# All branch gates through the front Strassen stage, both branch projections as a token-major Strassen stage

## The chip, the cores and the metric

One core of one Trainium2 chip. The metric is the device time of one execution of the whole program in microseconds (us). The kernel before takes 2709.2 us, the median of three runs (2709.17 to 2709.56).

## What is computed

One layer of a streaming encoder, 512 tokens wide (T), 2048 channels deep (D), all in float32:

```python
h = rmsnorm(x, norm_mix)
proj = h @ w_in
q_a, f_a, i_a, g_a, q_b, k_b, v_b, gate_a, gate_b = jnp.split(proj, IN_OFFSETS, axis=-1)
o_a = hgrn2_mixer(q_a, f_a, i_a, g_a, lb, hg_norm)      # 8 heads of 128: recurrence
o_b = swa_mixer(q_b, k_b, v_b, positions, sw_sinks)     # 16 query heads of 64, 4 key heads, window 128
merged = sigmoid(gate_a) * (o_a @ w_proj_a) + sigmoid(gate_b) * (o_b @ w_proj_b)
x = x + merged @ w_out
x = x + cross_attn(rmsnorm(x, norm_x), rmsnorm(mem, norm_mem))
x = x + (silu(hf @ w_gate) * (hf @ w_up)) @ w_down      # hf = rmsnorm(x, norm_ffn)
return rmsnorm(x, norm_final)
```

`w_proj_a` and `w_proj_b` are 1024x2048, `w_out` is 2048x2048, and each gate is 2048 channels wide.

## The kernel before

**Products.** A float32 product is made of three reduced products: each operand is split into a high part (a copy rounded to fp32r) and a low part (the rest), and `products` (L1024) issues low x high, high x low and high x high. ScalarE makes the high parts (`split_hi` L1733), GpSimd the low parts of the plainly computed weights (`split_lo` L917), VectorE those of the Strassen stages (`front_low`, `out_low_part`, `f_low`). Plain weights run through a ring of four slots (`w_raw`, `w_hi`, `w_lo`), one slot for a 128x1024 piece, a *chunk* of 24 matmuls with 512 columns (`chunk` L1034).

**Order.** Each engine has one instruction stream written out by hand; semaphores join them. SP issues the loads and GpSimd the accumulating loads, in the order in which each is written, so that a load stands behind every wait before it in its queue.

**Front stage** (`front_chunk` L1125, `front_high` L1803, `front_low` L2565, `front_combine` L2581). Part of `h @ w_in` is done as a Strassen product of 2x2 blocks: seven products in place of eight, each of 4 chunks of 12 matmuls, 28 chunks to a group of 1024 columns. There are NF = 4 groups: the first makes the values of branch A, groups 1 to 3 make 12 of the 16 column tiles of each gate. VectorE and ScalarE combine the blocks (`front_keep` L1840, `front_combine`), and SP stores them, not yet through the sigmoid, in DRAM (`front_store` L666).

**Heads.** The recurrence of the 8 heads follows (`head` L1188, L1920, L2622). In the last two head steps, which have no projections of their own, the four plain gate A tiles fill TensorE (`gate_ahead` L1184).

**Gate stage A** (`gate_stage` L1295, L1995; `gate_loads` L736; `gate_product` L2808). Sixteen times, one 128-column tile of `o_a @ w_proj_a` is computed with 24 matmuls, channels on partitions. For 12 of them the stored gate rows are loaded and turned by four transposes on TensorE, ScalarE takes the sigmoid, and VectorE writes gate times projection into `res`. Inside this stage, at tile 14, VectorE computes the angles of the rotary embedding (`rope_angles` L2792).

**Window attention** (L1380 to L1395; ScalarE from L2038; VectorE from L2855). 12 tiles of the projection: four of keys and values, each followed by its two tiles of queries, 48 matmuls each. Scores, softmax and values of a tile pair run in the middle of later chunks. At the end two plain gate B tiles stand.

**Gate stage B** is the same as A with `w_proj_b`; `merge` (L2892) adds to `res`. The other two plain gate B tiles stand in it.

**w_out** (`out_chunk` L1421, `out_high` L2068, `out_low_part` L2903, operands at L2086, L2918, L2936) is a Strassen stage of 56 chunks of 12 matmuls, with the channel-major `res` as its stationary side. Then come cross-attention, the feed-forward network and the last norm, which the change leaves alone but for semaphore names.

Of the kernel before, what the change touches and what calls it, by code (L numbers as in the profile page):

```python
# [24 lines left out]
P = 128  # L25
D = 2048
T = 512
# [27 lines left out]
C_K, C_V, C_H, C_GA, C_S, C_GB, C_XQ, C_XO, C_F = 0, 8, 16, 64, 88, 112, 136, 144, 152  # L55
# [3 lines left out]
NF = 4  # L59
FRONT = 28 * NF  # L60
FRONT_SETS = [(0, 2, 1), (1, 2, 0)] * (NF // 2)
PLAIN = 4
GATED = KT - PLAIN

# [14 lines left out]
def gate_chunk(m, stage):  # L79
    return (4, 7)[m] if m < 2 and stage else 8 + m  # L80
# [20 lines left out]
F0, TOTALS = FRONT, 4 * NF + OUT_SUMS  # L101
# [79 lines left out]
def build_trunk(nc, a, out):  # L181

    ctx = ExitStack()
    with ctx:
# [19 lines left out]
        res = at("res", 64 * KB, [P, KT, T], F32)  # L204
# [4 lines left out]
        o_lo = at("o_lo", 112 * KB, [P, HEADS, T], F32R)  # L209

# [47 lines left out]
        gate_t = at("gate_t", SCR + 25.5 * KB, [P, 2, T], F32)  # L258

        eps_col = stat[:, 31:32]  # L260
        gate_rows = at("gate_rows", SCR + 16 * KB, [P, 4, TT, P], F32)

# [37 lines left out]
        pos_i = at("pos_i", SCR + 12 * KB, [P, T], I32)  # L300
# [5 lines left out]
        out_last = [at(f"out_last{x}", (32 + 4 * x) * KB, [P, 2 * 512], F32) for x in range(4)]  # L306
        out_low = [at(f"out_low{x}", (48 + 4 * x) * KB, [P, 2 * 512], F32) for x in range(4)]
# [89 lines left out]
        gate_dram = nc.dram_tensor("gate_scratch", [2, TT, P, GATED * P], F32, kind="Internal").ap()  # L397
# [56 lines left out]
        def front_loaded(x, c, count):  # L454
            earlier = sum(1 for s in range(C_H + HC) if s % RING == c) if x == 0 else 0
            return 16 * (earlier + count)

# [71 lines left out]
        def front_block(n, p, c):  # L529

            left = BLOCK[p] in ("b11", "b21")
            c0 = I_A + (0 if left else 512) if n == 0 else (GATE_A if left else GATE_B) + 512 * n
            k0 = 2 * c + (0 if BLOCK[p] in ("b11", "b12") else CK)
            return w_rows[:, k0:k0 + 2, c0:c0 + 512]
# [15 lines left out]
        def front_freed(x):  # L550
            return max(i for i in range(FRONT) if front_slot(i) == x) + 1

# [20 lines left out]
        def w_slot_freed(eng, s):  # L573

            if C_XQ <= s < C_XQ + RING:
                last = max(k for k in range(NO) if k % RING == s % RING)
# [7 lines left out]
        def _(sp):  # L584
# [53 lines left out]
            for c in range(4):  # L638
                front_load(0, 5, c)
# [13 lines left out]
            for c in range(4):  # L653
                sp.wait_ge(w_lo_ready, max(s for s in range(C_H + HC) if s % RING == c) + 1)
                front_load(0, 0, c)
# [10 lines left out]
            def front_store(n, name):  # L666
# [5 lines left out]
                else:  # L672
                    sp.wait_ge(S("f_combined"), made(n, name))
# [62 lines left out]
            def gate_loads(gate0, w_proj, s0, stage):  # L736

                def project(m0, s, v=0, k=0):
                    unit(w_proj, m0, s, v, k, chunks=1)

                for m in range(2 if stage else PLAIN):
                    unit(w_in, gate0 + m * P, s0 + 2 * m)
                for m in range(2):
                    project(m * P, s0 + gate_chunk(m, stage))
                    if stage:
                        unit(w_in, gate0 + (2 + m) * P, s0 + gate_chunk(m, stage) + 1)
                if stage:
                    sp.wait_ge(S("sw_o_done"), HEADS)
                else:
                    sp.wait_ge(S("o_split"), HEADS)  # L750
                    for name in ("11", "12", "21", "22"):
                        sp.wait_ge(S(STORES[name]), front_stored(NF - 1))
                with sp.Fori(0, 3) as i:
                    for x in range(4):
                        project(i * (4 * P) + (2 + x) * P, s0 + gate_chunk(2 + x, stage), i, 4)
                        sp.wait_ge(S("turned"), i * 4 + (2 * KT + GATED * stage + x - 3))
                        sp.sem_inc(S("slot_free"), 1)
                        rows = gate_dram[stage][:, :, bass.ds(i * (4 * P) + x * P, P)].rearrange("t p d -> p t d")
                        sp.dma_start(gate_rows[:, x], rows).then_inc(S(f"x_in{x}"), 16)
                project(14 * P, s0 + gate_chunk(14, stage))  # L760
                project(15 * P, s0 + gate_chunk(15, stage))

            gate_loads(GATE_A, a["w_proj_a"].rearrange("l d n -> (l d) n"), C_GA, 0)
            for g in range(SWKV):
                s = C_S + 6 * g
# [7 lines left out]
                for x in range(2):  # L773
                    unit(w_in, Q_B + (2 * g + x) * P, s + 2 + 2 * x)
            gate_loads(GATE_B, a["w_proj_b"].rearrange("l d n -> (l d) n"), C_GB, 1)
# [5 lines left out]
            for j in range(4):  # L781
                sp.wait_ge(w_lo_ready, C_XQ - RING + j + 1)
                out_load(0, 0, j // 2, j % 2)
            sp.wait_ge(chunk_done, C_GB + 22)
# [23 lines left out]
            sp.wait_ge(S("x_o_done"), XH)  # L808
# [105 lines left out]
        def _(pool):  # L914
            pool.memset(ones[:, :], 1.0).then_inc(S("ones_set"), 1)
# [27 lines left out]
            for s in range(C_GA + LEAD, C_GA + RING):  # L943
                pool.wait_ge(w_lo_ready, s)
                split_lo(s)
            with pool.Fori(C_GA // RING + 1, C_XQ // RING) as i:
                for s in range(RING):
                    split_lo(s, i, RING)

# [73 lines left out]
        def _(pe):  # L1023
# [43 lines left out]
            for u in range(XH):  # L1067
# [5 lines left out]
                if u == 2:  # L1073

                    pe.wait_ge(S("ones_set"), 1)
# [49 lines left out]
            def front_chunk(i):  # L1125

                n, p, c = front_step(i)
                o = (pair[(0, 3)[n % 2]], pair[1], pair[(0, 3)[n % 2]], pair[1], pair[(0, 3)[n % 2]], pair[2], pair[(0, 3)[n % 2]])[p]
# [2282 lines left out]
```

## Time and profile before

| | |
|---|---|
| median of three runs | 2709.2 us |
| the profiled execution, span of its trace | 2707.3 us |
| TensorE busy | 2680.3 us (99%), 12902 matmuls |
| VectorE, ScalarE, GpSimd busy | 62%, 48%, 22% |
| DMA | 441.57 MB, 163 GB/s on average |

Busy time of an engine is the time in which an instruction of it runs; TensorE's matmuls are pipelined, so their own durations overlap, and the distance between two of them is read from a count in a stretch. Of each wait the profile names what ended it.

### The profile page before, as it was taken

What the parts mean: (1) busy time and instruction counts of PE and PEld (TensorE: products, weight loads), DVE (VectorE), ACT (ScalarE), POOL (GpSimd) and SP (SyncE); (2) the same over time, 40 slices, a digit from 0 to 9 for tenths busy, and PEclk for the clock granted to TensorE, in tenths of its full rate; (3) what the DMA queues carried; (4) which work ended last, traced back from release to release, by engine and by line L of the source; (5) the groups of instructions that cost most, each with busy time, mean ns of one, the idle gap of its engine ahead of it and who ended that gap; (6) DMA issues with size and microseconds to landing.
All of it is one profiled execution on the core that took longest, in us unless ns stands there. A gap on an engine that the chain in (4) does not pass through costs nothing.

```text
span 2707.3 us, 33905 instructions
## 1 busy us (share of the span) xinstructions
PE 2680.3 (99%) x12902; PEld 2225.3 (82%) x12902; DVE 1683.3 (62%) x2031; ACT 1306.9 (48%) x1634; POOL 601.6 (22%) x394
## 2 busy tenths in 40 slices
PE   8999999999999999999999999999999999999998
PEld 7878888888888888878887888888888888888887
DVE  5865557777413541488558556666555667778787
ACT  6544445545423552345455544444444445545446
POOL 7121110000233334311141221111122212121311
PEclk9999999999999999999999999999999999999999
DMA  8788884222153323586348787877778888898975
GB/s 279 207 197 199 191 186 114 86 83 83 55 160 93 79 79 111 158 214 147 110 148 216 169 176 166 192 179 171 178 166 177 170 217 193 198 209 236 188 213 134
DMA packets 356893, 441.57 MB, mean 163 GB/s; under 512 B 30265, under 2 KB 200593, under 8 KB 354193
## 3 DMA queue, kind: packets, MB, share of 16 engines
q1 hardware_dynamic: 277120, 286.23, 34.0%
q0 software_dynamic: 76704, 147.87, 31.9%
q10 hardware_dynamic: 2928, 5.56, 0.6%
q8 instruction: 93, 1.52, 0.2%
q14 instruction: 48, 0.39, 0.0%
HBM read 407.36 MB, written 32.24 MB: 162 GB/s over the span
## 4 chain that ended last, share of the span: by engine, by line
PE 88%; DMA 4%; issue 3%; DVE 3%; POOL 1%; ACT 1%; SPq 0%; DVEq 0%; POOLq 0%; ACTq 0%
PE psum L1027 17%; PE psum L1029 17%; PE psum L1028 17%; PE psum L1409 9%; PE psum L1410 9%; PE psum L1411 9%; PE psum L1160 2%; PE psum L1161 2%; PE psum L1162 2%; DMA f_raw<-in_w_down 1%; PE psum L1210 1%; PE psum L1649 1%; DMA f_raw<-in_w_out 1%; DMA fr_raw<-in_w_in 1%; DVE x_nat L2504 0%
## 5 line engine op out<-in xcount | busy, mean ns | idle before, releaser
L3132 DVE TENSOR_TENSOR f_lo<-f_raw,f_hi 128x1024 fp32r<-128x1024 f32 x458 | 559.4, 1225 | 398.2 <-ACT f_hi L2246 397.0
L2246 ACT ACTIVATE f_hi<-f_raw 128x1024 fp32r<-128x1024 f32 x460 | 486.8, 1061 | 620.6 <-PE psum L1411 311.6
L922 POOL TENSOR_TENSOR w_lo<-w_raw,w_hi 128x1024 fp32r<-128x1024 f32 x103 | 250.9, 2446 | 702.5 <-ACT w_hi L1739 700.4
L981 POOL DMA_DIRECT2D f_raw<-in_w_up x132 | 159.0, 1205 | 661.9 <-DVE f_lo L3132 656.2
L1027 PE MATMUL psum<-op_hi,w_lo 128*128 128x512 f32 x704 | 284.2, 404 | 0.0
L1029 PE MATMUL psum<-op_hi,w_hi 128*128 128x512 f32 x704 | 274.8, 390 | 0.0
L1028 PE MATMUL psum<-op_lo,w_hi 128*128 128x512 f32 x704 | 274.6, 390 | 0.0
L2568 DVE TENSOR_TENSOR fr_lo<-fr_raw,fr_hi 128x1024 fp32r<-128x1024 f32 x112 | 137.0, 1225 | 125.0 <-ACT fr_hi L1815 125.0
L1815 ACT ACTIVATE fr_hi<-fr_raw 128x1024 fp32r<-128x1024 f32 x112 | 118.5, 1061 | 167.4 <-PE psum L1162 82.4
L1739 ACT ACTIVATE w_hi<-w_raw 128x1024 fp32r<-128x1024 f32 x152 | 158.8, 1054 | 40.2 <-PE psum L1029 16.2
L1029 PEld LDWEIGHTS psum<-op_hi,w_hi 128*128 128x128 f32 x704 | 132.1, 188 | 28.5
L1027 PEld LDWEIGHTS psum<-op_hi,w_lo 128*128 128x128 f32 x704 | 132.5, 188 | 25.8 <-issue 0.9
L1028 PEld LDWEIGHTS psum<-op_lo,w_hi 128*128 128x128 f32 x704 | 132.6, 188 | 24.5 <-issue 0.2
L1000 POOL DMA_DIRECT2D f_raw<-in_w_down x70 | 86.0, 1444 | 285.6 <-DVE f_lo L3132 277.4
L1409 PE MATMUL psum<-f_hi,pa_lo 128*128 128x512 f32 x352 | 137.2, 390 | 0.6 <-DVE f_lo L3132 0.6
L1409 PE MATMUL psum<-f_hi,s_lo 128*128 128x512 f32 x352 | 137.0, 389 | 0.0
L1411 PE MATMUL psum<-f_hi,s_hi 128*128 128x512 f32 x352 | 137.0, 389 | 0.0
L1410 PE MATMUL psum<-f_lo,pa_hi 128*128 128x512 f32 x352 | 137.0, 389 | 0.0
L1410 PE MATMUL psum<-f_lo,s_hi 128*128 128x512 f32 x352 | 136.9, 389 | 0.0
L1411 PE MATMUL psum<-f_hi,pa_hi 128*128 128x512 f32 x352 | 136.9, 389 | 0.0
L1027 PE MATMUL psum<-f_hi,a_lo 128*128 128x512 f32 x344 | 134.8, 392 | 0.0
L1029 PE MATMUL psum<-f_hi,a_hi 128*128 128x512 f32 x344 | 134.0, 390 | 0.0
(438 smaller groups left out, 6282.8 us busy)
## 6 DMA issues: line engine op xcount, KB each, us to landing
f_raw<-in_w_up POOLq DMA_DIRECT2D x132, 512.0 KB, 6.5
f_raw<-in_w_gate SPq DMA_DIRECT2D x88, 512.0 KB, 4.2
w_raw<-in_w_in SPq DMA_DIRECT2D x80, 512.0 KB, 4.0
f_raw<-in_w_down POOLq DMA_DIRECT2D x70, 512.0 KB, 8.9
f_raw<-in_w_down SPq DMA_DIRECT2D x66, 512.0 KB, 5.6
fr_raw<-in_w_in SPq DMA_DIRECT2D x48, 512.0 KB, 4.6
fr_raw<-in_w_in POOLq DMA_DIRECT2D x48, 512.0 KB, 7.1
f_raw<-in_w_up SPq DMA_DIRECT2D x44, 512.0 KB, 4.6
```

The lines of the kernel that those rows point to most:

```text
L922: pool.tensor_tensor(w_lo[:, slot], w_raw[:, slot], w_hi[:, slot].bitcast(F32), ALU.subtract).then_inc(w_lo_ready, 1)
L981: pool.dma_start(raw_pieces(x, slot), up_block(n, p, c), accum_op=ALU.add).then_inc(raw_added[c], 16)
L1027: pe.matmul(b[:, 0:n], wl, xh, start=start, stop=False)
L1028: pe.matmul(b[:, 0:n], wh, xl, start=False, stop=False)
L1029: return pe.matmul(b[:, 0:n], wh, xh, start=False, stop=stop)
L1409: pe.matmul(b, lo[:, kt, f], w[0], start=False, stop=False, skip_group_check=True)
L1410: pe.matmul(b, hi[:, kt, f], w[1], start=False, stop=False, skip_group_check=True)
L1411: return pe.matmul(b, hi[:, kt, f], w[0], start=False, stop=stop, skip_group_check=True)
L1739: act.activation(w_hi[:, slot], w_raw[:, slot], ACT.Copy).then_inc(w_hi_ready, 1)
L2246: act.activation(f_split(i)[0][:, :], split_source(i)[:, :], ACT.Copy).then_inc(f_hi_ready, 1)
L2568: dve.tensor_tensor(fr_lo[front_slot(i)][:, :], front_source(i)[:, :], fr_hi[front_slot(i)][:, :].bitcast(F32), ALU.subtract).then_inc(f_l ...
L3132: dve.tensor_tensor(lo[:, :], split_source(i)[:, :], hi[:, :].bitcast(F32), ALU.subtract).then_inc(f_lo_ready, 1)
```

## The change

- **Gates.** NF = 5: all 16 tiles of each gate go through the front stage, 512 columns of gate A and 512 of gate B to a group. ScalarE takes the sigmoid there (`open_gate`), before the store. No plain gate tile is left, and the 24 x 4 transposes of gate rows go.
- **Keys ahead.** The four key/value tiles fill the last two head steps in place of the gate A tiles; ScalarE keeps them in `kv_raw`. The window attention that follows has the 8 query tiles alone. `rope_angles` stands on VectorE directly behind the last head.
- **Mixed stage.** Both projections become one Strassen stage with tokens on partitions: NG = 4 groups (side A and B, two column halves of 1024 each), each of 7 products x 2 chunks (YC = 14) of 12 matmuls. The stationary blocks and sums of `o_a`, `o_b` are made on VectorE (side A) and on GpSimd (most of side B). The sums of weight blocks are made in SBUF by GpSimd (`sum_blocks`, eight of 128x1024 a group). VectorE makes the low part of each chunk, the combinations, and gate times projection into `rows_m`. The rest of the window attention stands between the first five mixed chunks.
- **One turn.** The merged rows are turned once for `w_out`: 32 transposes between chunks of mixed group 3, 32 behind the first four chunks of `w_out` (`turn_merged`); ScalarE copies them into `res` (`merged_keep`).
- `w_out` uses its ring slots in another order (`out_slot`), and several semaphores are joined or renamed.

The diff, cut to its core:

```diff
-NF = 4
+NF = 5
...
+NG, YC = 4, 14
+MIXED = NG * YC
...
+def mixed_slot(i):
+    return (0, 2, 3)[i % FR]
+
+
+def out_slot(k):
+    return (3, 0, 2, 1)[k % RING]
...
+            def sum_blocks(o, other, waits):
+                for semaphore, count in waits:
+                    pool.wait_ge(semaphore, count)
+                pool.tensor_tensor(o[:, :], o[:, :], other[:, :], ALU.add).then_inc(S("m_summed"), 1)
...
+            for n in range(NG):
+                for c in range(2):
+                    sum_blocks(m_tot[n % 2][c], m_b12[c], ((f_lo_ready, mixed_at(n, 0) + c + 1), (S("m_b12_in"), 32 * (n + 1))))
+                for c in range(2):
+                    sum_blocks(m_tot[n % 2][c], m_b22[c], ((f_lo_ready, mixed_at(n, 1) + c + 1), (S("m_b22_in"), 32 * (n + 1))))
+                if n == 0:
...
+                    next_difference(ma_run, OA12, "m_raw")
+                if n == 1:
...
+                    difference(mb_run, OB21, OB22, "m_raw")
+                if n == 2:
+                    difference(mb_last, OB11, OB21, "m_last_raw")
+                for c in range(2):
+                    sum_blocks(m_b22[c], m_b12[c], ((f_lo_ready, mixed_at(n, 3) + c + 1),))
+                for c in range(2):
+                    sum_blocks(m_tot[n % 2][c], m_b21[c], ((f_lo_ready, mixed_at(n, 2) + c + 1), (S("m_b21_in"), 32 * (n + 1))))
...
+            def mixed_chunk(i):
+
+                n, p, c = mixed_step(i)
...
+                pe.wait_ge(f_lo_ready, FRONT + i + 1)
+                hi, lo = MIXED_STAT[n // 2][p]
+                for j in range(2):
+                    kt = 2 * c + j
...
+                    for t in range(2):
+                        xh, xl = [x[:, kt, t * P:(t + 1) * P] for x in (hi, lo)]
+                        if p in (0, 1, 5):
+                            last = products(o[:, t], 512, (xh, xl), (wh, wl), kt == 0, kt == 3)
...
+            def turn_merged(kt, b):
+                for t in range(TT):
+                    last = pe.transpose(bank[b][:, t * P:(t + 1) * P], rows_m[:, t, kt * P:(kt + 1) * P], ident[:, :])
+                last.then_inc(S("merged_turned"), 1)
...
+            mixed_chunk(0)
+            sw_turn(HEADS - 2)
+            sw_scores(HEADS - 1)
+            mixed_chunk(1)
+            sw_values(HEADS - 2)
+            mixed_chunk(2)
+            mixed_chunk(3)
+            sw_turn(HEADS - 1)
+            mixed_chunk(4)
+            sw_values(HEADS - 1)
...
             for k in range(NO):
                 out_chunk(k)
+                if k < 4:
...
+                    for y in range(2):
...
+                        turn_merged((12, 14, 8, 10)[k] + y, (2, 2, 0, 0)[k] + y)
...
+            def open_gate(n, name):
+
+                tile = FRONT_TILES[name]
+                act.wait_ge(S("f_combined"), made(n, name))
+                act.activation(tile[:, :, :], tile[:, :, :], ACT.Sigmoid).then_inc(S("gate_open"), 1)
...
-            gate_stage(C_GB, KT, 1)
             out_operand_high(0)
             out_high(0)
+            for x in (8, 9):
+                merged_keep(x)
             out_high(1)
+            for x in (10, 11):
+                merged_keep(x)
             out_operand_high(1)
...
             for k in range(2, NO):
                 out_high(k)
+                if k in (2, 3):
+                    for x in (8 + 2 * k, 9 + 2 * k):
+                        merged_keep(x)
...
+            dve.memset(kT_pad[:, 0:64], 0.0)
+            dve.memset(vT_pad[:, 0:64], 0.0)
+            rope_angles()
...
+            def gate_side(n, name, tile):
...
+                if n < 2:
+                    dve.wait_ge(S("gate_in"), 16 * 8)
+                    dve.tensor_tensor(o, o, tile, ALU.mult).then_inc(S("m_gated"), 1)
+                else:
...
+                    link(dve.tensor_tensor(g, g, tile, ALU.mult))
+                    dve.tensor_tensor(o, o, g, ALU.add).then_inc(S("m_gated"), 1)
...
+            for i in range(6, MIXED):
+                mixed_low(i)
+                mixed_outputs(i)
```

## Rows read from the trace of the kernel before

**Rows 1.** The page's first part: busy time, share of the span, instructions.

```profile
PE 2680.3 (99%) x12902; PEld 2225.3 (82%) x12902; DVE 1683.3 (62%) x2031; ACT 1306.9 (48%) x1634; POOL 601.6 (22%) x394
```

**Rows 2.** Waits of TensorE: us in total, times, longest.

```profile
PE psum L1409 <- DVE f_lo L2907: 1.3, 2, 1.0
```

**Rows 3.** Stretches: length, busy PE PEld DVE ACT POOL, clock, DMA share, GB/s.

```profile
0.00:10.00 10.00, 2.79 (x13) 2.68 (x14) 1.15 (x4) 3.18 (x7) 0.40 (x5) 1.00 0.77 245
200.00:360.00 160.00, 160.00 (x708) 132.47 (x707) 86.61 (x72) 70.28 (x68) 30.09 (x25) 1.00 0.85 198
741.00:1120.00 379.00, 379.00 (x2188) 311.32 (x2187) 118.35 (x221) 145.48 (x302) 146.20 (x62) 1.00 0.39 107
1137.00:1184.00 47.00, 45.14 (x196) 36.02 (x195) 36.83 (x33) 21.42 (x22) 14.47 (x12) 1.00 0.91 193
2700.00:2707.00 7.00, 0.00 (x0) 0.00 (x0) 1.94 (x7) 1.97 (x5) 0.00 (x0) 0.70 0.73 300
```

**Rows 4.** Chain that ended last: start, us, what.

```profile
741.41 0.86 PE psum L1261 x2
...
1500.02 0.87 PE psum L1649 x8
```

**Rows 5.** The page's part 5: costliest groups, VectorE and ScalarE.

```profile
L3132 DVE TENSOR_TENSOR f_lo<-f_raw,f_hi 128x1024 fp32r<-128x1024 f32 x458 | 559.4, 1225 | 398.2 <-ACT f_hi L2246 397.0
...
L1815 ACT ACTIVATE fr_hi<-fr_raw 128x1024 fp32r<-128x1024 f32 x112 | 118.5, 1061 | 167.4 <-PE psum L1162 82.4
```

**Rows 6.** Timelines of VectorE, ScalarE, GpSimd, 745 to 853 us: start, us, what.

```profile
745.95 0.69 DVE L2754 TENSOR_TENSOR o_lo<-o_t,o_hi 128x512 fp32r<-128x512 f32 x1 [0.78 <-ACT o_hi L1961]
...
772.69 2.39 POOL L922 TENSOR_TENSOR w_lo<-w_raw,w_hi 128x1024 fp32r<-128x1024 f32 x1 [3.54 <-ACT w_hi L1739]
...
835.85 0.11 DVE L2826 MEMSET kT_pad<- 128x64 f32 x1
...
846.12 0.43 DVE L2806 TENSOR_SCALAR turns<-q_rot 128x512 f32<-128x512 f32 x1
...
846.58 0.63 ACT L2024 ACTIVATE cos_t<-turns 128x512 f32<-128x512 f32 x1 [3.73 <-DVE turns L2806]
...
851.52 0.59 ACT L2059 ACTIVATE vT_pad<-psum 64x512 f32<-64x512 f32 x1 [2.41 <-PE psum L1029]
...
852.13 1.19 ACT L2063 ACTIVATE swapped_t<-psum 32x512 f32<-32x512 f32 x2
```

**Rows 7.** Timelines of TensorE, VectorE, ScalarE, 884 to 901 us: one tile pair's attention.

```profile
884.39 1.10 PE L1334 MATMUL psum<-kT_pad,q_rot 64*64 64x128 f32 x32
...
892.57 0.69 DVE L2852 TENSOR_TENSOR probs_t<-probs_t,sw_small 128x512 f32<-128x512 f32 x1
...
898.57 1.15 PE L1353 MATMUL psum<-probs_T,v_win 128*64 128x64 f32 x32
...
899.77 0.60 ACT L2051 ACTIVATE o_hi<-psum 128x512 fp32r<-128x512 f32 x1 [2.33 <-PE psum L1353]
```

**Rows 8.** Timelines of VectorE and GpSimd, 1387 to 1408 us.

```profile
1387.90 2.48 DVE L2968 TENSOR_TENSOR x_row<-x_row,psum 128x512 f32<-128x512 f32 x4 [2.96 <-PE psum L1029]
...
1389.10 2.41 POOL L922 TENSOR_TENSOR w_lo<-w_raw,w_hi 128x1024 fp32r<-128x1024 f32 x1 [3.03 <-ACT w_hi L1739]
...
1390.30 5.77 DVE L2995 TENSOR_TENSOR h_nat<-x_row,g_row 128x512 f32<-128x512 f32 x4
...
1393.11 2.41 POOL L972 TENSOR_TENSOR first_lo<-f_raw,first_hi 128x1024 fp32r<-128x1024 f32 x1 [1.60 <-ACT first_hi L2246]
...
1406.62 1.29 DVE L2995 TENSOR_TENSOR h_nat<-x_row,g_row 128x512 f32<-128x512 f32 x2
```

**Rows 9.** Timeline of TensorE, 3 to 24 us.

```profile
7.50 3.68 PE L1062 MATMUL psum<-ident,mem_nat 128*128 128x128 f32 x16 [4.29 <-DMA mem_nat<-in_mem]
...
16.13 0.41 PE L1027 MATMUL psum<-mem_hi,w_lo 128*128 128x256 f32 x1
...
17.00 0.28 PE L1027 MATMUL psum<-mem_hi,w_lo 128*128 128x256 f32 x1
```

More of the change, by code:

```diff
@@ L575, in w_slot_freed @@
             if C_XQ <= s < C_XQ + RING:
-                last = max(k for k in range(NO) if k % RING == s % RING)
+                last = max(k for k in range(NO) if out_slot(k) == s % RING)
                 eng.wait_ge(f_chunk_done, F0 + last + 1)
@@ L734, in _ @@
                     head_loads(i * 2 + (2 + x), C_H + 2 * HC + HC * x, x, i, 2 * HC)
[L736 to L763, printed above, removed]
             for g in range(SWKV):
-                s = C_S + 6 * g
+                s = C_KV + 2 * g
                 for j in range(2):
@@ new lines, in _, with pool_link, plain, difference @@
+            pool_links = [1]
+            def pool_link(ins):
+                ins.then_inc(S("pool_step"), 1)
+                pool_links[0] += 1
+                pool.wait_ge(S("pool_step"), pool_links[0])
+            def plain(block):
+                return [t.bitcast(F32) for t in block]
+            def difference(o, one, other, signal):
+                (hi1, lo1), (hi2, lo2) = plain(one), plain(other)
+                pool_link(pool.tensor_tensor(o[:, :, :], hi1, hi2, ALU.subtract))
+                pool_link(pool.tensor_tensor(o[:, :, :], o[:, :, :], lo1, ALU.add))
+                pool.tensor_tensor(o[:, :, :], o[:, :, :], lo2, ALU.subtract).then_inc(S(signal), 1)
@@ new lines, in swap_halves, with swap_keys @@
+            def swap_halves(src, m, rows):
+                before(act, S("q_roped"), m - (m + 2) // 3)
+                before(act, S("k_roped"), (m + 2) // 3)
+                for r in range(0, rows, 32):
+                    last = act.activation(swapped[r ^ 32:(r ^ 32) + 32, :], src[r:r + 32, :], ACT.Copy)
+                last.then_inc(S("halves_swapped"), 1)
+            def swap_keys(g):
+                before(act, S("windows_turned"), g)
+                act.wait_ge(S("lb_shifted"), 1 + 2)
+                act.activation(vT_pad[64:128, 64:64 + T], kv_raw[g][64:128, :], ACT.Copy).then_inc(S("vT_padded"), 1)
+                swap_halves(kv_raw[g], 3 * g, 64)
@@ new lines, in _ @@
+            for n in range(HEADS):
+                if n >= 2:
+                    turned_probs(n - 2)
+                if n >= 1:
+                    sw_max(n - 1)
+                if n % 2 == 0:
+                    turn_keys(n // 2)
+                if n >= 2:
+                    sw_out_low(n - 2)
+                if n % 2:
+                    copy_windows(n // 2)
+                if n >= 1:
+                    sw_normalise(n - 1)
+                if n == HEADS - 1:
+                    dve.wait_ge(f_lo_ready, FRONT)
+                    mixed_low(0)
+                    mixed_low(1)
+                done(C_S + 2 * n + 1)
+                turn_queries(n)
```

847 lines of the change are left out of this document (538 added, 309 removed).

## The prediction

> **What bounds the kernel now.** I read the page first: TensorE is busy for 99% of the span [rows 1]. Then the waits of TensorE: the part that changes has one entry there, two waits of 1.3 us in all for VectorE's low parts of the w_out weights [rows 2]. Then a table of stretches: in the front stage and in the one stretch from gate A over the window attention to gate B TensorE has no idle time at all, while VectorE, ScalarE and GpSimd are busy for little over half of it at most; only the start of the w_out stage loses 1.9 us of 47 [rows 3]. So in every stretch that the change touches the end is set by the number of matmuls, and the other three engines work in their shade. Two prices follow: 708 matmuls in 160 us, so **0.226 us** for a matmul of 512 columns (the 390 ns of the page overlap) [rows 3], and 8 transposes in 0.87 us, 0.109 us each [rows 4].
>
> **Work that goes.** The fifth front group adds 7 products x 4 chunks x 12 = 336 matmuls. The 8 gate tiles computed plainly go, 8 x 48 = 384. The projections take 4 groups x 14 chunks x 12 = 672 where 32 tiles x 24 = 768 stood. Net -144, x 0.226 = **-32.5 us**. Transposes: 24 gate tiles x 4 = 96 go, 16 merged tiles x 4 = 64 come, -32 x 0.109 = -3.5 us. Together **-36.0 us** on TensorE. The fifth group should run like the others: TensorE full at a DMA share of 0.85 [rows 3]. In the front stage ScalarE gets four sigmoids a group, and SP's stores of gates wait for them; behind these stores stand loads of the next group, which are wanted several chunks later, and ScalarE is busy for 70 us of 160 there, so I cost this at nothing. If that cover fails, the price is one activation of about 1.06 us [rows 5] per group, 5 us. The renamed semaphores cost nothing.
>
> **The rope angles lose their cover: +5.1 us.** Before, they were computed inside the gate A stage. Now VectorE does them after the last head, and ScalarE's splits for the third query chunk stand behind the two sines. From the rows: the mean product of the last head ends at 742.27 [rows 4]; key chunk 7 and the two query chunks split ahead take 3 x 24 x 0.226 = 16.3 us, so TensorE wants the third at 758.5. VectorE ends the last head at 746.64; the angles take 10.7 us (835.85 to 846.55), to 757.3; cosine 0.63, V copy 0.59, two half copies 1.19, split 1.06, GpSimd's low part 2.39 and some 0.4 of hand-overs (an estimate, four of about 0.1) give 763.6 [rows 5, 6].
>
> **The end of the attention: +4.3 us.** The first mixed chunk follows the seventh query tile directly; before, gate chunks stood there. Its low part stands on VectorE behind the softmax of pair 7. From scores to normalised probabilities a pair takes 884.39 to 893.26, 8.9 us [rows 7]; with the low part, 1.22 [rows 5], 10.1 us. TensorE has for it the scores and values, 1.1 each [rows 7], eight small transposes, at most 0.87 [rows 4], and half a chunk, 2.7: 5.8 us. Difference 4.3.
>
> **The mixed stage: the port that VectorE and GpSimd share.** This is the large term. Where GpSimd runs a split, VectorE operations with both inputs in SBUF stand still: four gain products, which take 0.65 each elsewhere, took 5.77 us while two GpSimd splits of 2.41 ran; four sums with one input in PSUM took 2.48 beside the first of these splits, undisturbed [rows 8]. So the two kinds exclude each other, and their times add. Before, GpSimd's splits run where VectorE has little of that kind to do. The mixed stage puts eight GpSimd sums of 128x1024 into each group beside VectorE's 14 low parts, operand sums and gate products, all with both inputs in SBUF. No row shows an in-place sum on GpSimd: below, it could cost VectorE nothing; above, it holds the port for a whole split, 2.39 us [rows 6]. I take the upper end, since the nearest row has the same engine, shape and two SBUF inputs. Per group, VectorE at 1.22 an operation, TensorE at 168 x 0.226 = 38.0 us:
> - n=0: GpSimd 10 x 2.39 = 23.9; VectorE 14 low parts, 8 operations for the sums of side A, 4 low parts of these, 2 gates, 28 x 1.22 = 34.2; with 9 us of attention work in VectorE's queue, during which GpSimd mostly waits for a low part that stands behind it, 67 us. TensorE has 38.0 and 5 of attention: **+24**.
> - n=1: 13 x 2.39 + 18 x 1.22 = 53.1: **+15.1**. The sums of side B for GpSimd are five of the 13.
> - n=2: 11 x 2.39 + 24 x 1.22 = 55.6 (two operations for a gate product from here on): **+17.6**.
> - n=3: 8 x 2.39 + 21 x 1.22 = 44.7, against 38.0 and 32 transposes of merged rows, 3.5: **+3.2**.
>
> Sum +60. VectorE's combinations with PSUM are left out, since they can run beside GpSimd. Loads are no bound: SP brings 4 MB in 50 us where the front stage has more. SP's loads of a group wait for sums and low parts of the one before, and the gate rows of B stand in the same queue, but all are asked for several chunks ahead.
>
> **The start of w_out: +14.2 us, less 1.9.** In the first four chunks TensorE transposes two merged tiles after each chunk, and ScalarE's split for the next chunk stands behind the copies of these tiles. So after each pair: copy 0.60, split 1.06, VectorE's low part 1.22, hand-overs 0.15, 3.0 us in which TensorE has nothing [rows 5, 7]. Before chunk 2 an operand split (1.06) and VectorE's gate product stand in between, 5.2. Together 3 x 3.0 + 5.2. The 1.9 us that this stretch loses now [rows 3] go, as its added transfers get a longer lead.
>
> **Sum.** -36.0 + 5.1 + 4.3 + 60 + 14.2 - 1.9 = +45.7 on the span of 2707.3, 2753.0; the median of the runs shown is 1.9 above that span, so **2755 us**, slower by 1.7%. A measurement of this kernel can tell about 0.2%, 5.4 us, from no change.
>
> **Rivals.**
> 1. *The in-place sums don't hold the port, and the mixed stage runs at TensorE's pace.* Its place is the whole mixed stage, its price 0 for the 60; then -36.0 + 5.1 + 4.3 + 14.2 - 1.9 = -14.3, 2695 us, **faster**. The attention work at the stage's start alone (VectorE 34.2 + 9 + 2.4 of combinations, 45.6, and pair 8's scores, softmax and values in series) can bring some 12 us back, 2707. It decides when the mixed stage stalls for less than 14 us. For it: every row of exclusion is with a split or a gain, none with an in-place sum. Against: same engine, same shape, both inputs in SBUF. Chance 0.17, of that 0.11 for faster and 0.06 for no change.
> 2. *The clock falls in the new stalls.* At the start, after idle time, 16 transposes take 3.68 us, 0.23 each where 0.109 is usual, and products of 256 columns last 0.41 at 16.1 us and 0.28 from 17 us on [rows 9], though the table gives a granted clock of 1.00 there; in the last 7 us, when TensorE has nothing to do, it is 0.70, a mixture of the two levels, 2.4 and 1.2 GHz [rows 3]. So an idle time may be followed by half the pace from 7.5 to about 16.5 us, 9 us, of which 4.5 are lost. I forecast five stalls near 5 us or above (rope, start, two in the first group, chunk 2 of w_out): 5 x 4.5 = 22, of which some 5 hide where the port is the bound anyway, so +17, 2772 us. Against: the kernel's inner waits now are too short to show anything. Chance 0.14. On this the Trainium skill ("TensorE: Matmul & The Clock Gate", section "Why this matters for your kernels") advises against idle gaps between bursts of matmuls, because the clock then goes back to its half rate. By that rule this rival would be the forecast, some 17 us above the sum; the trace agrees only at its two ends.
> 3. *The front stage doesn't take the fifth group for the price of a matmul count* (a sigmoid or a store late in each group, 5 us, on top of the forecast): 2760; chance 0.06, within the forecast's own spread.
>
> **The numbers.** Forecast 0.63, rival 1 0.17, rival 2 0.14, rival 3 0.06. The forecast's own spread is some 15 us either way, 2740 to 2770, since the port's terms hang on the order in which the two engines take turns. The range reaches up past rival 2, to 2782, and down to 2712, which takes in a port that costs a third of what I reckon and leaves out rival 1. Slower 0.83, within 0.2% 0.06, faster 0.11.
>
> **What would show it.** In the profile after: TensorE's share falls from 99% to some 96%; its waits name VectorE's low part of the mixed weights; GpSimd's sums, or VectorE's low parts, last well over 2.4 and 1.22 us wherever both run; stalls of 3 us in front of w_out's chunks 1 to 4; one of 5 us before the third query chunk. Wrong would be: low parts of 1.22 us beside running GpSimd sums, a mixed stage of about 160 us for the four groups, or matmuls spaced 0.43 us after a stall.

## The result, and the profile after

The changed kernel takes **2768.4 us**, the median of its four executions, against 2709.4 for the kernel before: ratio **1.0211**, 95% interval 1.0197 to 1.0225. One of the four took 3848.7 us at a mean granted clock of 0.653 and is left out of the ratio; the other three took 2764.9 to 2769.5. Forecast was 2755 in a range from 2712 to 2782, slower with 0.83. The profiled execution has a span of 2765.4 us, 58.1 above that of before; the sum of the forecast had 45.7.

The page after, its busy times and the row of granted clocks, which answer to [rows 1]:

```profile
PE 2670.8 (97%) x12726; PEld 2206.5 (80%) x12726; DVE 1884.8 (68%) x2128; ACT 1370.6 (50%) x1692; POOL 623.1 (23%) x400
...
PEclk9999999999999989999999999999999999999999
```

TensorE has 176 matmuls and transposes less, as counted (144 and 32), and is busy for a smaller share of a longer span. The waits of TensorE after (us in total, times, longest), where [rows 2] had one entry of 1.3:

```profile
PE psum L1182 <- DVE m_lo L3177: 19.8, 12, 5.0
PE psum L1563 <- DVE m_lo L3177: 16.0, 14, 5.4
PE psum L1182 <- DVE f_lo L3289: 15.0, 6, 5.4
PE psum L1182 <- POOL w_lo L1028: 8.7, 3, 4.4
PE psum L1182 <- ACT sw_small L2233: 7.9, 1, 7.9
```

The two lines of `m_lo` are the low parts of the mixed weights, `f_lo` those at the start of w_out, `w_lo` is GpSimd's low part at two places, `sw_small` the softmax of the last query tile. Three of these waits, at the entry of the heads, at the first mixed chunk and at the third (start, us, what, in brackets the wait):

```profile
494.29 0.77 PE L1182 MATMUL psum<-op_hi,w_lo 128*128 128x512 f32 x1 [3.85 <-POOL w_lo L1028]
954.30 0.76 PE L1182 MATMUL psum<-m_hi,o_lo 128*128 128x512 f32 x1 [4.96 <-DVE m_lo L3177]
972.76 0.80 PE L1182 MATMUL psum<-m_hi,ms_lo 128*128 128x512 f32 x1 [7.95 <-ACT sw_small L2233]
```

Where the waits stand is shown by the table of stretches (columns as in [rows 3]): front; heads; attention; the four groups of the mixed stage; w_out as far as the point (a short wait that both kernels have) from which both run alike.

```profile
0.00:490.40 490.40, 479.08 (x2222) 398.61 (x2222) 293.26 (x270) 244.39 (x264) 121.75 (x84) 1.00 0.81 205
490.40:826.20 335.80, 331.95 (x1674) 279.59 (x1674) 228.58 (x563) 175.79 (x225) 24.24 (x10) 0.99 0.32 89
826.20:954.30 128.10, 118.76 (x906) 96.50 (x904) 84.44 (x164) 78.73 (x207) 33.97 (x15) 0.97 0.24 71
954.30:1020.50 66.20, 50.91 (x280) 39.95 (x281) 59.04 (x51) 26.69 (x43) 31.20 (x11) 0.85 0.45 159
1020.50:1073.10 52.60, 43.58 (x169) 33.24 (x168) 45.33 (x23) 19.25 (x19) 38.44 (x13) 0.94 0.28 93
1073.10:1127.30 54.20, 43.24 (x170) 32.71 (x169) 52.81 (x29) 19.25 (x19) 32.09 (x11) 0.94 0.25 85
1127.30:1173.80 46.50, 42.92 (x201) 34.50 (x200) 38.05 (x26) 21.32 (x25) 20.28 (x8) 1.00 0.27 91
1173.80:1275.80 102.00, 84.01 (x370) 67.16 (x368) 74.79 (x66) 44.92 (x49) 16.63 (x14) 0.98 0.74 187
```

Two things are to be seen. VectorE is busy for some 80 to 97% of the mixed groups, where it was busy for a third of the comparable stretch of the kernel before [rows 3]. And the granted clock is below 1.00 in every stretch behind the front stage but the fourth mixed group, whose longest wait is 2.0 us. Behind the wait of 4.37 us at the third query chunk the matmuls follow one another at 0.43 us instead of 0.23 (846.97, 847.53, 847.96 below): TensorE runs at the lower of its two levels, 1.2 instead of 2.4 GHz.

```profile
846.97 0.77 PE L1182 MATMUL psum<-op_hi,w_lo 128*128 128x512 f32 x1 [4.37 <-POOL w_lo L1028]
847.53 0.63 PE L1183 MATMUL psum<-op_lo,w_hi 128*128 128x512 f32 x1
847.96 0.63 PE L1184 MATMUL psum<-op_hi,w_hi 128*128 128x512 f32 x1
```

In the mixed stage VectorE and GpSimd take turns. The second group's timelines of the two (start, us, what):

```profile
1023.74 1.21 DVE L3209 TENSOR_TENSOR rows_m<-rows_m,psum 128x1024 f32<-128x1024 f32 x1
...
1036.35 6.76 DVE L3177 TENSOR_TENSOR m_lo<-m_b,m_hi 128x1024 fp32r<-128x1024 f32 x2
...
1022.76 5.67 POOL L1059 TENSOR_TENSOR m_tot<-m_tot,m_b 128x1024 f32<-128x1024 f32 x2 [2.30 <-DVE m_lo L3177]
...
1035.42 3.27 POOL L1074 TENSOR_TENSOR mb_run<-mb_run,ob_lo 128x1024 f32<-128x1024 f32 x1
1038.77 3.26 POOL L1075 TENSOR_TENSOR mb_run<-mb_run,ob_lo 128x1024 f32<-128x1024 f32 x1
```

Two low parts of 1.22 us each take 6.76 while GpSimd runs two operations of about 2.4, each of which takes 3.26: nearly 1.22 + 2.4 for each pair. The product with one input in PSUM takes 1.21 beside a running sum. Over the whole stage, 25 of the 56 low parts meet no GpSimd operation and take 1.21 to 1.23 us; the 31 that meet one take 1.21 to 3.46, with a median of 3.24.

### The profile page after: what moved, and what is told of

Read it like the earlier page. It is cut to its first block, busy times and chain, and to the rows that moved or that the text cites. A ratio compares the mean times of both kernels' runs of the same rounds, so it can differ in the third digit from the quotient of the medians.

```text
span 2765.4 us, 33259 instructions
## 1 busy us (share of the span) xinstructions
PE 2670.8 (97%) x12726; PEld 2206.5 (80%) x12726; DVE 1884.8 (68%) x2128; ACT 1370.6 (50%) x1692; POOL 623.1 (23%) x400
## 4 chain that ended last, share of the span: by engine, by line
PE 73%; issue 11%; DVE 6%; POOL 5%; DMA 3%; ACT 2%; SPq 0%; POOLq 0%; ACTq 0%; DVEq 0%
PE psum L1182 13%; PE psum L1184 13%; PE psum L1183 13%; PE psum L1604 8%; PE psum L1606 8%; PE psum L1605 8%; PE psum L1315 2%; PE psum L1316 2%; PE psum L1317 2%; DMA f_raw<-in_w_down 2%; DVE m_lo L3177 1%; POOL w_lo L1028 1%; POOL f_raw L1155 1%; PE psum L1365 1%; PE psum L1857 1%
## 5 line engine op out<-in xcount | busy, mean ns | idle before, releaser
L2868 DVE TENSOR_TENSOR fr_lo<-fr_raw,fr_hi 128x1024 fp32r<-128x1024 f32 x140 | 171.3, 1225 | 159.2 <-ACT fr_hi L2021 159.2
L1028 POOL TENSOR_TENSOR w_lo<-w_raw,w_hi 128x1024 fp32r<-128x1024 f32 x55 | 136.1, 2490 | 547.4 <-ACT w_hi L1947 546.8
L2021 ACT ACTIVATE fr_hi<-fr_raw 128x1024 fp32r<-128x1024 f32 x140 | 148.3, 1061 | 200.0 <-PE psum L1317 100.6
L1182 PE MATMUL psum<-op_hi,w_lo 128*128 128x512 f32 x576 | 235.9, 410 | 8.2 <-POOL w_lo L1028 8.2
L1183 PE MATMUL psum<-op_lo,w_hi 128*128 128x512 f32 x576 | 226.7, 394 | 0.0
L1184 PE MATMUL psum<-op_hi,w_hi 128*128 128x512 f32 x576 | 226.6, 393 | 0.0
L1040 POOL DMA_DIRECT2D fr_raw<-in_w_in x60 | 72.4, 1207 | 312.8 <-DVE fr_lo L2868 302.1
L1183 PE MATMUL psum<-f_lo,a_hi 128*128 128x512 f32 x344 | 133.9, 389 | 0.0
L1182 PEld LDWEIGHTS psum<-op_hi,w_lo 128*128 128x128 f32 x576 | 109.7, 190 | 29.5 <-issue 9.2
L1184 PEld LDWEIGHTS psum<-op_hi,w_hi 128*128 128x128 f32 x576 | 109.4, 190 | 23.9
```

The costliest lines, as they stand in the source:

```text
L1028: pool.tensor_tensor(w_lo[:, slot], w_raw[:, slot], w_hi[:, slot].bitcast(F32), ALU.subtract).then_inc(w_lo_ready, 1)
L1182: pe.matmul(b[:, 0:n], wl, xh, start=start, stop=False)
L1183: pe.matmul(b[:, 0:n], wh, xl, start=False, stop=False)
L1184: return pe.matmul(b[:, 0:n], wh, xh, start=False, stop=stop)
L2021: act.activation(fr_hi[front_slot(i)][:, :], front_source(i)[:, :], ACT.Copy).then_inc(f_hi_ready, 1)
L2868: dve.tensor_tensor(fr_lo[front_slot(i)][:, :], front_source(i)[:, :], fr_hi[front_slot(i)][:, :].bitcast(F32), ALU.subtract).then_inc(f_l ...
```

## The experiments

All spans are compared with 2765.4 of the changed kernel, from which each edit starts. "Heads" is from the last front matmul to the last pair of matmuls of the heads' mean squares (335.2 us after), "attention" from there to the first mixed chunk (129.1), "w_out" from its first matmul to the point from which both kernels run alike (102.0; before 80.9). All but the last two kernels were executed once. Where an edit leaves a stretch alone, it still differs from run to run: heads 334.1 to 335.3, attention 128.3 to 129.9, the first mixed group 66.2 to 68.3, w_out 100.3 to 105.4. So a gain is read from its own stretch and not from the span.

### Slot order of the front stage

```diff
 def front_slot(i):
-    return (0, 2, 3)[i % FR]
+    return (3, 0, 2)[i % FR]
```

> One thing: the three slots of the front stage's splits are used in the order 3, 0, 2 and not 0, 2, 3, so that the slot of the first head's weights is free three chunks before the end of the stage and not with its last chunk. Theory (140 chunks are 2 more than a multiple of 3, 112 were 1 more, so the fifth group moved the last use of that slot to the last chunk): ScalarE's first split of the head weights goes from 490.6 to about 485, the wait of 3.85 us of TensorE at the entry of the heads goes, and with it the half pace behind it; the heads' stretch takes 329 us in place of 335.8, the span falls by about 6.9. If the clock had nothing to do with the wait: 3.9 less. Rival (the split is late because ScalarE stands behind the last sigmoid, or its load is late): nothing changes.

Heads took **328.8** us in place of 335.2, the wait and the half pace behind it were gone; the span fell by 4.9 to 2760.5, since w_out, with the same waits, took 104.8 this time. ScalarE's first split of the heads' weights, after and here:

```profile
490.61 1.06 ACT L1947 ACTIVATE w_hi<-w_raw 128x1024 fp32r<-128x1024 f32 x1 [6.27 <-issue]
```

```profile
484.10 1.06 ACT L1947 ACTIVATE w_hi<-w_raw 128x1024 fp32r<-128x1024 f32 x1 [0.83 <-issue]
```

The cause is shown, since only the order of the slots differs: neither sigmoids nor stores are late. A stage of 140 chunks ends on another slot than one of 112, and the next stage's first weights need that slot.

### The second query tile's splits ahead of the sines

```diff
             keep_keys(2)
             keep_keys(3)
+            for x in range(2):
+                split_hi(C_S + LEAD + x)
```

> One thing: ScalarE splits the weights of the second query tile before the two sines and not behind them and the copies of the first keys. Theory (the split stands in ScalarE's queue behind the angles of VectorE): the wait of 4.37 us before the third query chunk goes, and the 2.4 us that TensorE loses behind it at half pace; some of it can come back as a wait for the first scores, whose keys and queries still hang on the angles, up to 2 us. Span 4 to 7 us less. Rival (GpSimd or the load is what is late): no change. If the half pace comes from elsewhere, the matmuls there are still 0.43 us apart with no wait ahead of them.

A miss. The wait at the chunk went, and one as long came at the first scores; attention took 129.6, the span 2770.7. The waits of TensorE in this run:

```profile
PE psum L1458 <- DVE q_rot L3166: 4.2, 1, 4.2
```

ScalarE's queue only hands on that the angles are late.

### The angles in VectorE's idle time

```diff
-            head(9, 1, project=False, mix=False, chain=False)
...
-            dve.memset(kT_pad[:, 0:64], 0.0)
-            dve.memset(vT_pad[:, 0:64], 0.0)
             rope_angles()
+            head(9, 1, project=False, mix=False, chain=False)
+            dve.memset(kT_pad[:, 0:64], 0.0)
+            dve.memset(vT_pad[:, 0:64], 0.0)
```

The buffer `turns` moves to a place that the heads no longer use.

> VectorE computes the rotary angles before the end of the last head, in the 16.4 us in which it waited for ScalarE's root there, and their buffer lies elsewhere; the two memsets stay where they were. Theory (the angles on VectorE are what is late, the split behind them in ScalarE's queue only passes it on): the wait of 4.37 us goes with the half pace behind it, no wait for the first scores comes in its place, the span falls by 6 to 7 us. Rival (the key copies, the swaps and GpSimd are as late by themselves): a wait of over 2 us stays at the third query chunk or at the first scores.

Attention took **123.0** us in place of 129.1, with no wait of 0.5 us in it; the span fell by 8.0 to 2757.4. With the run before: the angles are the cause.

### Work in place of the idle time

```diff
                     pe.wait_ge(S("o_scaled"), HEADS)
+                    for x in range(18):
+                        pe.matmul(bank[2], op_hi[:, 0, 0, 0:P], op_tokens(op_hi, 0), start=True, stop=True)
```

> Puts 18 matmuls of 512 columns, whose result nobody reads, ahead of the third query chunk, where TensorE waited 4.37 us: 18 x 0.227 = 4.1 us of work in place of idle time. Clock theory (the idle time is what halves the pace behind it): the chunk starts within 0.3 us of where it did, its matmuls follow one another at 0.227 us and not at 0.43, and TensorE is 2.4 us earlier from there on; the granted clock of the 10 us behind it is 1.00 in place of 0.91. Rival (the half pace belongs to that place, loads or the change of operands): matmuls still 0.43 us apart behind the fill.

TensorE's timeline of this run:

```profile
841.46 4.24 PE L1511 MATMUL psum<-op_hi 128*128 128x512 f32 x18
845.96 0.50 PE L1182 MATMUL psum<-op_hi,w_lo 128*128 128x512 f32 x1 [0.26 <-POOL w_lo L1028]
846.29 0.40 PE L1183 MATMUL psum<-op_lo,w_hi 128*128 128x512 f32 x1
846.53 0.39 PE L1184 MATMUL psum<-op_hi,w_hi 128*128 128x512 f32 x1
```

Same weights, same loads, same place: behind 4.24 us of useless matmuls the chunk runs at 0.23 us a matmul, behind 4.37 us of nothing at 0.43. The ten us behind the chunk's start have a granted clock of 0.76 after and of 1.00 here:

```profile
847.00:857.00 10.00, 10.00 (x34) 8.06 (x35) 5.22 (x5) 5.64 (x7) 5.72 (x3) 0.76 0.36 105
```

```profile
846.00:856.00 10.00, 10.00 (x76) 8.07 (x76) 5.73 (x7) 5.66 (x7) 5.72 (x3) 1.00 0.37 107
```

Attention took 127.3 us, 1.8 less than after and 1.0 less than the shortest of the runs that leave it alone; my 2.4 was too much, and the granted clock of the longer stretch that I had quoted, 0.91, was that of 850 to 860. That the idle time halves the pace is shown.

### The start of w_out

```diff
             out_operand_high(0)
             out_high(0)
+            out_high(1)
             for x in (8, 9):
                 merged_keep(x)
-            out_high(1)
+            out_high(2)
             for x in (10, 11):
                 merged_keep(x)
+            out_high(3)
             out_operand_high(1)
```

VectorE's low parts move in the same way.

> One thing: at the start of w_out the high and low parts of chunks 1 to 4 stand one place earlier in the queues of ScalarE and VectorE, ahead of the copies of the merged tiles of the chunk before, and of the gate products. Theory (the splits stand behind these copies): the four waits of 2.9, 5.4, 2.9 and 3.0 us go, with the half pace behind the second; what is left is under 3 us; the stretch from the first w_out chunk to where both kernels run alike takes 86 us in place of 102, the span falls by 14 to 17. Rival (the raw blocks or the accumulating loads are late, so the splits wait for data): the waits stay, with ScalarE waiting for a DMA.

W_out took **87.7** in place of 102.0, the span fell by 14.8 to 2750.6. Of the line of `f_lo`, 15.0 us in six waits, this is left, more than the 3 us that I expected:

```profile
PE psum L1182 <- DVE f_lo L3295: 4.3, 2, 2.9
```

The queue order is the cause, as forecast; the data were there.

### GpSimd writes and doesn't read

```diff
-                pool.tensor_tensor(o[:, :], o[:, :], other[:, :], ALU.add).then_inc(S("m_summed"), 1)
+                pool.memset(o[:, :], 0.0).then_inc(S("m_summed"), 1)
```

> Leaves out the sums of the weight blocks: GpSimd writes zeros over the 128x1024 tile in place of adding two tiles, so it reads nothing; every wait and every VectorE instruction is as before. Port theory (two GpSimd inputs from SBUF exclude VectorE's two-input operations): VectorE's low parts of the mixed weights are all near 1.22 us, and with 8 x 2.39 us a group off the port the mixed stage falls from 219.5 us to 165 to 185, and the span by 35 to 55. Chain theory (sum, split, low part and chunk follow one another for each tile, whatever the port does): if the write takes as long as the sum the stage stays near 219; if it is shorter, the stage falls by that difference on the chain, some 16 links, while low parts beside it are 1.22 us. VectorE theory (its own instructions are too many for the stage): no change beyond 5 us.

Spans: 2742.3, 23.1 less. The mixed stage took 193.2 us, between my bounds of the port theory, 165 to 185, and those of the chain theory, by which 16 links of 2.39 less 0.95 leave some 196. The low parts and the writes (ns, least, median, largest), and the four groups:

```profile
L3177 DVE TENSOR_TENSOR m_lo<-m_b,m_hi x24: 1216/1225/3425, 992.6 to 1136.5; 128x1024 fp32r<-128x1024 f32 x24
...
L1059 POOL MEMSET m_b<- x8: 951/952/955, 993.8 to 1123.5; 128x1024 f32 x8
```

```profile
953.50:1017.70 64.20, 49.33 (x280) 39.64 (x281) 47.09 (x52) 26.68 (x43) 14.91 (x11) 0.87 0.47 164
1017.70:1060.50 42.80, 40.31 (x170) 32.55 (x169) 31.98 (x23) 19.26 (x19) 22.90 (x13) 0.96 0.31 102
1060.50:1104.70 44.20, 41.20 (x169) 33.46 (x168) 38.62 (x28) 19.39 (x19) 17.37 (x11) 0.92 0.35 116
1104.70:1146.70 42.00, 41.99 (x201) 34.76 (x200) 29.56 (x26) 21.39 (x25) 6.56 (x7) 1.00 0.31 100
```

The median of these 24 low parts, which read `m_b`, was 3.23 us in the changed kernel and is 1.225 here; that of the other 32, which read `m_tot`, is 1.22 in both. GpSimd's stationary sums of side B still read here, and the five low parts that stay above 1.5 us all run beside one of these; the nine that run beside a write take 1.22 to 1.23:

```profile
1031.38 3.26 POOL L1074 TENSOR_TENSOR mb_run<-mb_run,ob_lo 128x1024 f32<-128x1024 f32 x1
1032.60 3.13 DVE L3177 TENSOR_TENSOR m_lo<-m_b,m_hi 128x1024 fp32r<-128x1024 f32 x1 [0.21 <-ACT m_hi L2277]
...
1039.71 1.84 POOL L1059 MEMSET m_tot<- 128x1024 f32 x2
1040.06 1.23 DVE L3177 TENSOR_TENSOR m_lo<-m_b,m_hi 128x1024 fp32r<-128x1024 f32 x1 [4.33 <-ACT m_hi L2277]
```

Groups 2 to 4 lose 9.8, 10.0 and 4.5 us; the first loses 2.0 only. Since a write also takes 0.95 us and not 2.39, a shorter chain could give some of this too: the run alone doesn't part the two.

### The sums on VectorE

```diff
+                if p in (0, 1, 3, 4):
+                    o, other, signal = {0: (tot, m_b12[c], "m_b12_in"), 1: (tot, m_b22[c], "m_b22_in"),
+                                        3: (m_b22[c], m_b12[c], "m_b12_in"), 4: (tot, m_b21[c], "m_b21_in")}[p]
...
+                    dve.tensor_tensor(o[:, :], o[:, :], other[:, :], ALU.add).then_inc(S("m_summed"), 1)
```

> The sums of the weight blocks move from GpSimd to VectorE, each right behind the low part that frees its tile; nothing is left out. Port theory (the two engines' times add): a sum holds the port for 1.22 us in place of 2.39, so groups 2 to 4 of the mixed stage, 52.6, 54.1 and 46.5 us, take 44 to 49, 46 to 51 and 42, the first stays within 3 us of 66; the span falls by 12 to 25. VectorE theory (its queue is what is too full): 8 x 1.22 more a group, the stage grows by 20 to 39 us. Chain theory alone, with no port: a link of sum, split and low part shortens from 2.39 to 1.22, gain of some 10 us, and low parts that were 3.2 us beside GpSimd's sums were not lengthened by them, so they stay long.

```profile
954.00:1018.30 64.30, 50.12 (x281) 40.21 (x282) 58.01 (x60) 26.69 (x43) 5.62 (x2) 0.84 0.47 164
1018.30:1067.60 49.30, 39.52 (x170) 31.11 (x169) 48.20 (x30) 19.36 (x19) 25.36 (x8) 1.00 0.26 83
1067.60:1111.70 44.10, 40.49 (x169) 32.44 (x168) 42.42 (x37) 19.26 (x19) 0.00 (x0) 0.96 0.35 122
1111.70:1156.80 45.10, 42.39 (x202) 34.72 (x201) 39.20 (x34) 21.39 (x25) 0.00 (x0) 1.00 0.29 94
```

Eight operations more on VectorE in each group, and each group is shorter: the span falls by 15.7 to 2749.7. Of my ranges only the span's holds: 49.3 us is just above its 44 to 49, 44.1 below 46 to 51, 45.1 above 42. The theory that VectorE has too many instructions of its own falls for groups 2 to 4 of the changed kernel; with the sums on it, VectorE is busy for 87 to 98% of them. What the two engines take together counts, and a sum costs half as much on VectorE.

### The first group: three runs

First VectorE's maxima of the last query tile moved ahead of three operations:

```diff
             turned_probs(HEADS - 2)
+            sw_max(HEADS - 1)
             mixed_difference(ma_run, OA21, OA22, "m_raw")
             mixed_low(2)
             mixed_sum_low(0, 1)
-            sw_max(HEADS - 1)
```

> VectorE takes the maxima of the last query tile's scores before the first stationary difference, the third low part and the first stationary low part, and not behind these 6.1 us. Theory (the first group is bound by the end of the attention in VectorE's queue, since the third chunk writes the banks in which these scores lie): the wait of 7.95 us at the third chunk falls to 4 to 5 us, where the low parts moved behind take over, the first group takes 62 to 63.5 us in place of 66.2. Port theory for this group too: the sums of GpSimd decide, and it stays within 1 us.

A miss: the wait went from 7.95 to 7.5 us, and the group took 69.3, no less than the 66.2 to 68.3 without the edit. ScalarE's exponentials still stood behind its two splits, which now waited longer for the difference. So the order was changed on both engines:

```diff
             turned_probs(HEADS - 2)
+            sw_exps(HEADS - 1)
+            sw_out_high(HEADS - 2)
             mixed_sum_high(0, 1)
             mixed_high(3)
-            sw_exps(HEADS - 1)
-            sw_out_high(HEADS - 2)
```

On VectorE the edit above stands, and `mixed_low(6)` goes ahead of the last difference.

> The first group of the mixed stage in another order, on both engines that the run before left one of: ScalarE takes the last tile's exponentials ahead of the first stationary split and the fourth chunk's split, VectorE the maxima ahead of the difference, and both the seventh chunk's split and low part ahead of the last stationary sum. Same work. Theory (this group is bound by the end of the attention and by what stands in these two queues, not by the port): the wait of 7.95 us at the third chunk falls to 4 to 5.5 us, that of 5.4 to 8.0 at the seventh to under 3, the group takes 56 to 60 us in place of 66 to 69, the other three stay within 1 us. Port theory for this group: within 2 us of 66.

A miss again: the group took 68.9 us. The wait at the third chunk fell to 4.7, as expected, but those of 0.85 and 5.4 behind it became 1.9, 1.3, 1.7 and 6.1; the sum of the waits rose from 14.2 to 15.7. What one gives another takes. So work was left out:

```diff
-                link(dve.tensor_tensor(o[:, :, :], hi1, hi2, ALU.subtract))
-                link(dve.tensor_tensor(o[:, :, :], o[:, :, :], lo1, ALU.add))
-                dve.tensor_tensor(o[:, :, :], o[:, :, :], lo2, ALU.subtract).then_inc(S(signal), 1)
+                dve.tensor_tensor(o[:, :, :], hi1, hi2, ALU.subtract).then_inc(S(signal), 1)
```

The same is done to `mixed_next`.

> Leaves out of VectorE's stationary sums the operations on the low parts: five of the eight of side A, all in the first seven chunks of the first group, and one of side B in the third group; every wait stays. VectorE theory for the first group (its queue, with the end of the attention, side A's sums and the low parts, is what sets these seven chunks, which took 45.2 us in which the matmuls of chunks and attention have some 24): 5 x 1.22 = 6.1 us less, the group takes 59 to 62 us in place of 66.2 to 69.3. Rival (the chain from scores over maxima, exponentials and values, or GpSimd's sums, set it): less than 2 us. Groups 2 to 4 within 1.5 us of 52.6, 54.1, 46.5.

```profile
952.10:1013.90 61.80, 52.02 (x280) 40.66 (x281) 51.46 (x46) 26.82 (x43) 31.18 (x11) 0.87 0.49 170
```

The group took **61.8**, 4.4 less than the 66.2 of after, the shortest of the runs that leave it alone, with GpSimd as busy as there (31.2 us). Five operations of VectorE decide more in it than all of GpSimd's weight sums, whose removal from GpSimd brought 2.0.

### All together

> All that helped, together: slot order of the front stage, angles early, block sums on VectorE, order at the start of w_out, order of the first group. If the places are independent, the stretches add: 2765.4 - 6.4 - 6.1 - 16.7 - 14.3 - 6 to 10 = 2712 to 2716 of span, less up to 5 for half pace behind waits that are gone: the kernel takes 2709 to 2718 us, within 0.35% of the one before, and does not beat it by more than 0.1%. If one gain hides another (the sums on VectorE make its queue the bound of the first group), 2718 to 2730.

Over five runs 2725.7 us (2724.6 to 2727.2), ratio to the kernel before **1.0050** (1.0036 to 1.0063). The stretches add up: heads -6.4, attention -6.1, mixed stage 205.4 for 219.5, w_out 86.9 for 102.0, in all -41.7 of 2765.4, and the span is 2723.9. The first of the two expectations was too low: the order of the first group gave nothing (65.6 us).

> As the run with all, and the eight operations of GpSimd on the stationary sums of side B go to VectorE too, so GpSimd computes next to nothing in the mixed stage. Port theory: 8 x (2.39 - 1.22) = 9.4 us less port time in groups 2 and 3, of which 5 to 9 come off the span: 2702 to 2712 us, ratio to the kernel before 0.998 to 1.001. VectorE theory: 8 x 1.22 = 9.8 us more, slower than the run with all by up to 10.

Over nine runs 2718.6 us (2716.5 to 2723.7), ratio **1.0028** (1.0018 to 1.0038): 7 us better than the run with all, as the port theory has it, but above the 2702 to 2712 that I gave. The second group of the run with all, and the four groups of this run:

```profile
1006.80:1057.60 50.80, 42.44 (x169) 33.33 (x168) 49.66 (x31) 19.38 (x19) 25.36 (x8) 0.93 0.28 91
```

```profile
940.30:1006.00 65.70, 50.34 (x280) 40.00 (x281) 57.35 (x60) 26.59 (x43) 6.50 (x2) 0.87 0.45 160
1006.00:1047.60 41.60, 39.19 (x169) 31.22 (x168) 40.40 (x35) 19.39 (x19) 0.00 (x0) 1.00 0.30 101
1047.60:1093.50 45.90, 40.95 (x169) 32.29 (x168) 45.35 (x40) 19.39 (x19) 0.00 (x0) 0.96 0.34 115
1093.50:1138.80 45.30, 42.41 (x202) 34.65 (x201) 39.36 (x34) 22.47 (x26) 0.00 (x0) 1.00 0.28 93
```

This parts the port from the chain of sum, split, low part and chunk: for the second group's weights that chain is the same in both runs, only the stationary sums of side B go from GpSimd into VectorE's queue, and the group falls from 50.8 to 41.6 us.

No version tried beats the kernel before. VectorE is now busy for 97 and 99% of the second and third groups, so its own work is likely what bounds them next; that was not tried. What is left is mostly the first group: 65.7 us where TensorE has 43, with GpSimd out of it.

## Why the prediction was right, and where it wasn't

**Matmul work, -36.0.** Right: the counts are met exactly, and the last matmul of the front stage comes 77.1 us later than before, where 336 matmuls at 0.226 us are 75.9.

**Entry of the heads, forecast 0, bound 5: 6.4.** Here a step failed: "ScalarE is busy for 70 us of 160 there, so I cost this at nothing". The load of ScalarE wasn't the question. The count of chunks was: the slot order ends elsewhere. 3.85 us of wait and 2.5 of half pace.

**Rope angles, forecast 5.1: 6.1.** Right in mechanism: a wait of 4.4, and 1.7 of half pace.

**End of the attention, forecast 4.3: 5.0.** Right in size, by the wait at the first mixed chunk. That the softmax in VectorE's queue is its cause was not tried by itself.

**Mixed stage.** By the forecast the four groups take 67, 53.1, 55.6 and 44.7 us (TensorE's 38 and what stands beside it, plus each term); measured 66.2, 52.6, 54.2 and 46.5. In the second and third groups the reason is shown too: in-place sums hold the port, the times of the two engines add, and taking GpSimd off it brought 41.6 us in the second and 44.1 in the third. In the fourth the gain was 1.2 to 4.5. **In the first the size was right by luck and the reason wrong**: "GpSimd 10 x 2.39 = 23.9" doesn't belong in that sum. Without the reads it took 64.2, without the sums on GpSimd 64.3 to 65.8. Its loss stands in the first seven chunks (45.2 us after), where the end of the attention and the stationary sums follow one another in the queues of VectorE and ScalarE. How much of that is the queue and how much the chain of dependent steps stays open.

**W_out, forecast 14.2 less 1.9, and 3.5 of transposes: 15.8; measured 21.1** (102.0 less 80.9). The four waits, 2.9, 5.4, 2.9 and 3.0, were forecast as 3.0, 5.2, 3.0 and 3.0. But the 1.9 us of before did not go (waits of 0.6, 0.9 and 0.5 us stand there), and the half pace took the rest.

**The clock, rival 2.** I made it a rival of 0.14 and should have put it in the sum. It came, but not at the 4.5 us a stall of the rival, and added less than 17 where it can be parted: 2.5 us at the heads, 1.7 at the angles, some 3 at w_out. In the second and third mixed groups it lies under the port's bound, and in the first, which has the lowest granted clock, 0.85, no run parts it from the waits; the mean granted clock, 0.990 for 0.999, allows 25 us in all (an estimate, 0.009 of the span). The Trainium skill ("TensorE: Matmul & The Clock Gate", section "Why this matters for your kernels") advises against such gaps; by it rival 2 was the forecast, and the fill run agrees with its rule (granted clock 1.00 for 0.76); two waits of 3.5 to 3.6 us, named in the last section, don't.

**Rival 1** (sums don't hold the port) fell: low parts with a median of 3.24 us wherever they meet GpSimd. **Rival 3** came in its size only, 6.4 for 5: behind the stage and not in each group, and from the slot order, not from a sigmoid or a store.

**The sum.** The span is 12.4 us above the forecast's. The entry of the heads, 6.4, and w_out, 5.3, make up nearly all of that; the other terms are each about 1 us off.

## What to carry to other kernels

Work moved to an engine in the shade is free only as long as its partner on the same port leaves room: for a stage in which VectorE and GpSimd both read pairs from SBUF, add their times, and put an operation where it is shorter. Price each new wait with the half pace behind it, and seek idle time of the late engine before reordering the queue that only hands a delay on. When a loop gets one more round, check which slot of each ring it ends on.

## What the runs showed of the hardware that I had not expected

- The half pace did not follow each wait of the same length. Behind 3.85, 4.37 and 5.40 us it came in every run that has these waits (granted clock 0.67 to 0.85 in the ten us from the end of the wait); behind the waits of 2.9 at w_out it came in some executions only. Nor is the order of lengths kept: behind a wait of 3.53 us (run e8_max_first, at 1096.6) and one of 3.58 (e5_vector_sums, at 1054.7) the granted clock stayed 1.00. With the same four waits w_out took between 100.3 and 105.4 us in ten kernels that left it alone.
- A GpSimd operation that only writes doesn't hold VectorE up: nine low parts of 1.22 to 1.23 us beside writes of 0.95. The Trainium skill ("SBUF — State Buffer", section "Who interferes with whom") says so: an operation of VectorE with two inputs in SBUF contends with a GpSimd instruction that reads SBUF, not with one that only writes it. The run agrees.
- GpSimd is held up as well: its 32 sums took 2.36 to 3.48 us, and the 24 of them into `m_tot` have a median of 3.30.
